# Two modulation spans of layer 2 computed by GpSimd and VectorE in place of TensorE

## The chip, the cores and the metric

One core of one Trainium2 chip runs the whole program in one launch. The metric is the time of an execution in microseconds, as the device measures it, of the slowest (here the only) core.

## The reference, cut to what matters

Four layers of a transformer-like block run one after another on 256 latent tokens and 256 context tokens, width 2048, in float32. In this text they are layers 0 to 3. Each layer is modulated by a condition vector:

```python
mod = jax.nn.silu(cond) @ w_ada[l] + b_ada[l]          # (2048) @ (2048, 6144)
shift, scale, gate = jnp.split(mod, 3, axis=-1)
h = rms_norm(x, norm_g[l]) * (1.0 + scale) + shift     # for latent and context tokens
p = h @ w_in[l]                                        # projections, attention, pooling, gates
x = x + gate * (merged(p) @ w_out[l])
```

There are two conditions for each layer (latent and context). Each third of a layer's w_ada, 2048 x 2048 numbers or 16.8 MB, is called a span here: span (2, 0) gives layer 2's shift, (2, 1) its scale, (2, 2) its gate. The modulation does not depend on x, so a span can be computed long before its layer begins. Layers 1 and 3 update only the latent tokens, so most of their projections run on 256 tokens; in layers 0 and 2 they run on 512.

## The kernel before, in words

**Slots.** All large weights pass through 500 slots of 128 x 1024 numbers (512 KB). SyncE's queue (SP) loads slot n into one of four w_raw buffers; ScalarE (`high`, line 732) copies it, rounded, to one of two w_high buffers; VectorE (`low`, line 1076) writes the rest, w_raw minus w_high, to w_low. TensorE forms each product as three matmuls (`three`, line 1670): high by high, low by high, high by low. While it computes slot n, the other two engines prepare slot n + 1. A w_high buffer is free when TensorE has used the slot two before (`slot_used`), so at the start of slot n ScalarE may begin on slot n + 1. A slot of 256 columns has 24 matmuls.

**Order.** `plan_phases` lists the phases of each layer, and every engine runs through the same list in its own program, in order. For layer 1 the slots are: q 120 to 135, kv to 143, cq to 151, ckv to 159, g_mla to 175, kr 176 and 177, g_gqa to 193, two short phases of the low-rank products to 207, then attention (mla) without slots, the splitting of its output (ysplit), and out 208 to 239. Beside cq, ckv and the first slot of g_mla runs another attention, one step a slot: TensorE scores, VectorE maximum, ScalarE exponential, VectorE weights, TensorE transposes and values. At the start of a layer (`root`, `apply`) VectorE scales x and writes h_low while TensorE begins on q. In out, each half round ends in a residual chain on VectorE: the update of x (line 1520), squares (1536), two sums (1542, 1550).

**Three forms for a span.** The modulation is done beside the slots in one of three forms, laid out by digits in the phases' lists.
- *Units* (`ada`, `span_unit`, line 1766): 16 units of 1 MB. For each, TensorE multiplies 4 x (128 x 512) numbers by the condition, and adds up in the PSUM bank `modulation` (AD). Units come in pairs behind the second and sixth slot of a round. `span_cols` (line 1775) turns the row into columns.
- *Mod pieces* (`mod`, `pieces`, lines 1120 and 1122): a span is two blocks of 16 pieces, 512 KB each. VectorE multiplies a piece by the condition and adds it to an accumulator, once for each of two conditions, two operations over 128 x 1024 a piece. At a block's end TensorE sums over partitions (`block_sums`, line 1787) and turns (`block_cols`, line 1821), ScalarE copies a row (line 752), VectorE adds the bias.
- *Gate pieces* (`gate`, `gate_pieces`, line 1140): the same for one condition only, one operation a piece.

Each queue is in order: SP loads piece p when VectorE has used piece p - 2, and the loads of later slots stand behind that wait. `TURNS` gives the bank AD to one owner at a time. In layer 1 before the change, q holds 8 units, kv and cq 4 each (span (2, 0)), and out 16 (span (2, 1)); kv, cq and ckv have 32 gate pieces. GpSimd only does the pooling of layers 2 and 3.

Of the kernel before, what the change touches and what calls it, by code (L numbers as in the profile page):

```python
# [8 lines left out]
P = 128  # L9
D = 2048  # L10
KC = D // P
S = 256
# [55 lines left out]
def plan_phases():  # L68
# [55 lines left out]
    for layer in range(LAYERS):  # L124
# [8 lines left out]
        if layer < 2:  # L133
            beside = 0 if layer == 0 else 1
            vec = (lambda m: m) if layer == 0 else (lambda m: "")
            late = (lambda m: m) if layer == 1 else (lambda m: "")
            linear("q", layer, 2, toks, "feat", "copy", "Q", heads=q_heads, ahead=5, ada=2 * beside,
                   mod=vec("0000000011111111"))
            linear("kv", layer, 1, ALL, "kv", "copy", "KV", ada=beside, mod=vec("11111210"), gate=late("11111111"), heads=all_stages({0: ("q", 3), 1: ("k", 0)}))
            att = attention(layer, 1, HD ** -0.5, 34, both)  # L140
            att["first"] = at["slot"]
            linear("cq", layer, 1, toks, "feat", "copy", "C", att=att, ada=beside, mod=vec("11111111"), gate=late("11111111"))
            linear("ckv", layer, 1, ALL, "feat", "copy", "C", att=att, off=2, mod=vec("11111111"), gate=late("22222222"))
            linear("g_mla", layer, 2, toks, "feat", "silu", "G", att=att, mod=vec("0111111111111111"))
            add("kr", layer=layer, att=att, mod=vec("10"))
# [3 lines left out]
            at["fd"] += 1  # L149
            linear("g_gqa", layer, 2, toks, "feat", "gate", "Q", sync=True, ranks="cq", mod=vec("1111121212111000"))  # L150

# [21 lines left out]
        else:  # L173
# [17 lines left out]
        add("ysplit", layer=layer, toks=toks)  # L191
        linear("out", layer, 4, toks, "feat", "res", "X", ada=4 if layer == 1 else 0, ahead=3,
               mod={0: "00011121121121110121121121121000", 2: "00000110110110111111121111111000"}.get(layer, ""))
# [14 lines left out]
def build(nc, dram, out):  # L208
# [7 lines left out]
    with ctx:  # L216
# [56 lines left out]
        pool_v = place("pool_values", [P, 2, PAD + S + PAD])  # L273
        pool_s = place("pool_sums", [P, 2, PAD + S + PAD])
        pool_edge = place("pool_edge", [P, 4, 2, 2, PAD])
        cols = place("gain_cols", [P, N_COLS])
# [33 lines left out]
        gate_used, gate_sum, gate_rowed = sem("gate_used"), sem("gate_sum"), sem("gate_rowed")  # L310
        gate_col, gate_ready = sem("gate_col"), sem("gate_ready")
        sq_done, ms_done, root_done = sem("sq_done"), sem("ms_done"), sem("root_done")
        scaled = sem("scaled")
# [41 lines left out]
        def columns_ready(layer, parts):  # L355

            if layer == 0 and parts == 2:
                return ada_ready, ADA_FIRST
            if (layer, parts - 1) in ADA_SPANS:
                return ada_ready, ADA_FIRST + ADA_SPANS.index((layer, parts - 1)) + 1  # L360
            if (layer, parts - 1) in GATE_SPANS:
# [109 lines left out]
        for ph in PH:  # L471
# [10 lines left out]
            for i in range(ph.get("ada", 0)):  # L482
# [3 lines left out]
                if span_of(q)[1] == 3:  # L486
                    TURNS.append((first, n0 + 8 * i + 8, "span", span_of(q)[0]))
        TURNS += [(n + 1, n + 3, "mod", b) for n, b in BLOCK_END.items()]
        TURNS.sort()
        for t, u in zip(TURNS, TURNS[1:]):  # L490
# [10 lines left out]
        def bank_free(kind, index):  # L501

            return turn_done(kind, index, dict(span=ada_ready, mod=mod_ready, gate=gate_ready))

        def row_free(kind, index):

            return turn_done(kind, index, dict(span=ada_col, mod=mod_col, gate=gate_col))

# [40 lines left out]
        def _(sp):  # L549
# [120 lines left out]
        def _(pool):  # L670
# [6 lines left out]
            def own():  # L677
                pool.wait_ge(own_pool, own_n[0])

            step(nc.gpsimd.memset(pool_v[:, :, :], 0.0))  # L680
            for ph in PH:
# [38 lines left out]
        def _(act):  # L720
# [24 lines left out]
            def block_row(n):  # L745
# [5 lines left out]
                act.wait_ge(mod_sum, b + 1)  # L751
                nc.scalar.copy(ada_row, AD[:, :]).then_inc(mod_rowed, 1)

            def gate_row(n):
# [181 lines left out]
            for pi, ph in enumerate(PH):  # L936
# [22 lines left out]
                elif kind == "linear":  # L959
# [41 lines left out]
                    def round_(i):  # L1001
# [3 lines left out]
                        for k in range(8):  # L1005
# [6 lines left out]
                            block_row(n0 + 8 * i + k)  # L1012
                            gate_row(n0 + 8 * i + k)
                            head_side(ph, 8 * i + k)
                            att_side(ph, n0 + 8 * i + k)
# [44 lines left out]
        def _(dve):  # L1060
# [81 lines left out]
            def gate_columns(n):  # L1142

                if n - 3 not in GATE_END:
# [288 lines left out]
            for pi, ph in enumerate(PH):  # L1433
# [37 lines left out]
                elif kind == "linear":  # L1471
# [95 lines left out]
                    def round_(i):  # L1567
# [3 lines left out]
                        for k in range(8):  # L1571
# [94 lines left out]
        def _(pe):  # L1666
# [112 lines left out]
            def block_sums(n):  # L1779
# [154 lines left out]
            for pi, ph in enumerate(PH):  # L1934
# [4 lines left out]
                elif kind == "linear":  # L1939
# [46 lines left out]
                    def round_(i):  # L1986
# [4 lines left out]
                        for k, (j, s) in enumerate(slot_plan(ph, i)):  # L1991
# [297 lines left out]
```

## Time and profile before

| | |
|---|---|
| median of 3 runs | 3003.23 us (2996.53 to 3004.24) |
| the profiled execution's own time | 3003.08 us |
| its span | 3001.3 us |
| its mean granted TensorE clock | 0.979 |
| TensorE busy | 2852.5 us (95%) |
| VectorE busy | 1910.9 us (64%) |
| ScalarE busy | 1024.4 us (34%) |
| GpSimd busy | 109.4 us (4%) |

The span is what the profiler saw from the first to the last instruction; the execution's time holds a little more around it. Engines stand in the rows as PE (TensorE matmuls), PEld (its weight loads), DVE (VectorE), ACT (ScalarE), POOL (GpSimd) and SP. A float32 matmul leaves two records. An arrow with an engine behind a time says what ended the wait.

### The profile page before, as it was taken

Reading aid. Unit: us, or ns where it says so; the run is one execution under the profiler, and the core shown is the slowest. Engines: PE = TensorE matmul, PEld = TensorE weight load, DVE = VectorE, ACT = ScalarE, POOL = GpSimd, SP = SyncE. Lnnn points to the kernel's source line nnn. Section 1 sums busy time; section 2 is a strip of 40 time slices with the busy share of each in tenths; the row PEclk is TensorE's granted clock in tenths of the full one; section 3 lists DMA queues with packets and bytes.
Section 4 is the critical chain, followed back from the end, with each engine's and each line's share of the span. In section 5 each row is a group of like instructions: output and inputs, shape, how many; then the busy total and the mean of one; then the engine's idle time right before and its main releaser. Section 6 shows DMA issues by size and latency. Waiting matters only on the chain.

```text
span 3001.3 us, 40313 instructions
## 1 busy us (share of the span) xinstructions
PE 2852.5 (95%) x16432; PEld 2350.3 (78%) x16432; DVE 1910.9 (64%) x2852; ACT 1024.4 (34%) x1515; POOL 109.4 (4%) x157
## 2 busy tenths in 40 slices
PE   6899999999998999999989999999999989999998
PEld 2588887786786888986877789767778877897888
DVE  3477677656887576455565577877576864538564
ACT  3223343225213233434332222334441232225463
POOL 0000000000000000000000000530000000004100
PEclk9999999999998999999999999999999989999999
DMA  9554344430555865434756755222534533322455
GB/s 404 233 175 163 122 153 143 159 116 36 180 199 178 288 228 183 160 114 143 275 189 234 265 212 183 104 91 106 181 120 156 182 111 123 97 92 91 151 180 169
DMA packets 145641, 501.90 MB, mean 167 GB/s; under 512 B 16048, under 2 KB 41392, under 8 KB 134960
## 3 DMA queue, kind: packets, MB, share of 16 engines
q1 hardware_dynamic: 136048, 489.65, 46.2%
q10 hardware_dynamic: 9408, 9.67, 0.9%
q8 instruction: 130, 2.13, 0.3%
q14 instruction: 55, 0.45, 0.1%
HBM read 484.05 MB, written 8.39 MB: 164 GB/s over the span
## 4 chain that ended last, share of the span: by engine, by line
PE 74%; DVE 8%; PEld 6%; issue 4%; DMA 3%; ACT 2%; POOL 1%; SPq 1%; PEldq 0%; DVEq 0%; ACTq 0%; POOLq 0%
PE products L1670 61%; PEld products L1670 5%; PE turned L1901 2%; DMA w_raw<-w_slots 2%; PE scores L1884 1%; DVE w_low L1076 1%; DVE tmp L1215 1%; PE modulation L1766 1%; ACT w_high L732 1%; DVE ada_w L1122 1%; PE products L1864 1%; DVE h_low L1243 1%; PEld turned L1901 1%; DMA mix_b<-ada_slots 1%; PE turned L1893 1%
## 5 line engine op out<-in xcount | busy, mean ns | idle before, releaser
L1670 PE MATMUL products<-h_high,w_high 128*128 128x512 f32 (+1 forms) x3424 | 1251.4, 365 | 84.3 <-DVE h_low L1243 33.0
L1670 PE MATMUL products<-h_low,w_high 128*128 128x512 f32 (+1 forms) x3424 | 1192.5, 348 | 0.0
L1670 PE MATMUL products<-h_high,w_low 128*128 128x512 f32 (+1 forms) x3424 | 1192.3, 348 | 0.0
L732 ACT CAST w_high<-w_raw 128x1024 fp32r<-128x1024 f32 x500 | 523.4, 1047 | 1327.0 <-PE products L1670 1135.9
L1076 DVE TENSOR_TENSOR w_low<-w_raw,w_high 128x1024 fp32r<-128x1024 f32 x500 | 614.5, 1230 | 557.5 <-ACT w_high L732 554.8
L1670 PEld LDWEIGHTS products<-h_high,w_high 128*128 128x128 f32 x3424 | 661.1, 193 | 254.7 <-issue 120.7
L1670 PEld LDWEIGHTS products<-h_low,w_high 128*128 128x128 f32 x3424 | 662.9, 194 | 79.4 <-issue 10.8
L1670 PEld LDWEIGHTS products<-h_high,w_low 128*128 128x128 f32 x3424 | 661.1, 193 | 81.1
L1122 DVE SCALAR_TENSOR_TENSOR ada_w<-ada_w,cond_silu 128x1024 f32<-128x1024 f32 x300 | 373.3, 1286 | 2.4 <-DMA ada_w<-mod_slots 0.7
L1670 PE MATMUL products<-w_high,h_high 128*128 128x256 f32 x640 | 183.3, 286 | 3.0 <-DVE w_low L1076 2.4
L1670 PE MATMUL products<-w_high,h_low 128*128 128x256 f32 x640 | 181.1, 283 | 0.0
L1670 PE MATMUL products<-w_low,h_high 128*128 128x256 f32 x640 | 181.1, 283 | 0.0
L891 ACT ACTIVATE tmp<-scores,softmax_stats,q_root 128x512 f32<-128x512 f32 (+1 forms) x144 | 101.4, 708 | 146.3 <-DVE softmax_stats L1363 146.3
L1670 PEld LDWEIGHTS products<-w_high,h_high 128*128 128x128 f32 x640 | 122.7, 192 | 7.5 <-issue 4.8
L1670 PEld LDWEIGHTS products<-w_high,h_low 128*128 128x128 f32 x640 | 122.8, 192 | 1.0 <-issue 1.0
L1670 PEld LDWEIGHTS products<-w_low,h_high 128*128 128x128 f32 x640 | 122.8, 192 | 0.0
L695 POOL COPY pool_values<-mix_a 128x512 f32<-128x512 f32 (+1 forms) x16 | 12.4, 773 | 2671.5 <-DVE mix_a L1509 2670.1
L1356 DVE TENSOR_REDUCE softmax_stats<-scores 128x1 f32<-128x512 f32 (+1 forms) x144 | 85.9, 597 | 30.1 <-PE scores L1881 19.2
L878 ACT COPY tmp<-turned 128x512 f32<-128x512 f32 (+1 forms) x96 | 49.3, 513 | 149.2 <-PE turned L1893 149.2
L810 ACT ACTIVATE h_high<-tmp,ada 128x256 fp32r<-128x256 f32 x128 | 57.5, 500 | 80.4 <-DVE tmp L1215 80.4
L1373 DVE RECIPROCAL softmax_stats<-softmax_stats 128x1 f32<-128x1 f32 x192 | 26.1, 157 | 65.5 <-ACT tmp L891 64.8
L1215 DVE SCALAR_TENSOR_TENSOR tmp<-x_residual,mod_scale,scores 128x256 f32<-128x256 f32 x128 | 55.2, 476 | 7.9 <-PE scores L1723 4.5
(232 smaller groups left out, 2698.7 us busy)
## 6 DMA issues: line engine op xcount, KB each, us to landing
w_raw<-w_slots SPq DMA_DIRECT2D x500, 512.0 KB, 3.7
ada_w<-mod_slots SPq DMA_DIRECT2D x160, 512.0 KB, 3.7
ada_w<-ada_slots SPq DMA_DIRECT2D x58, 1024.0 KB, 7.8
mix_b<-gate_slots SPq DMA_DIRECT2D x32, 512.0 KB, 4.0
mix_a<-gate_slots SPq DMA_DIRECT2D x32, 512.0 KB, 4.2
mix_a<-ada_slots SPq DMA_DIRECT2D x12, 1024.0 KB, 14.3
mix_b<-ada_slots SPq DMA_DIRECT2D x10, 1024.0 KB, 15.1
x_scratch<-x_residual ACTq DMA_DIRECT2D x3, 2048.0 KB, 9.1
```

Of the source, the lines that this page charges most:

```text
L732: nc.scalar.copy(whi[:, n % SPL, :], raw[:, n % RAW, :]).then_inc(high_done, 1)
L810: last = nc.scalar.activation(hh[:, t, tk], xs(t)[:, tk], ACT.Identity, bias=adaT[:, r, c + st:c + st + 1])
L878: nc.scalar.copy(dst[:, 0:nk], src[:, 0:nk]).then_inc(pt_done, 1)
L891: nc.scalar.activation(tmp[:, t0 + c % ring, 0:nk], src, ACT.Exp, scale=a["scale"] if a["wide"] else q_rs[:, k:k + 1], bias=stat[:, c % 8, ...
L1076: nc.vector.tensor_tensor(wlo[:, n % SPL, :], raw[:, n % RAW, :], whi[:, n % SPL, :].bitcast(F32), ALU.subtract).then_inc(low_done, 1)
L1122: ins = nc.vector.scalar_tensor_tensor(acc, w, c, acc, ALU.mult, ALU.add)
L1215: last = nc.vector.scalar_tensor_tensor(xs(t)[:, tk], xT[:, t, tk], mod_scale[:, t, st:st + 1], SC[:, 1, tk], ALU.mult, ALU.mult)
L1243: last = nc.vector.scalar_tensor_tensor(hl[:, t, tk], xs(t)[:, tk], adaT[:, r, c + st:c + st + 1], hh[:, t, tk].bitcast(F32), ALU.add, ALU ...
L1356: step(nc.vector.reduce_max(stat[:, c % 8, 0:1], src, AX.X))
L1670: ins = nc.tensor.matmul(o, a, b, start=first and q == 0, stop=last and q == 2, skip_group_check=skip)
L1766: ins = nc.tensor.matmul(AD[32 * j:32 * j + 32, :], sc32[:, k, :], place[:, j * 512:(j + 1) * 512], start=k == 0, stop=k == KC - 1)
L1901: ins = nc.tensor.matmul(o, v[:, kt, hc * HD:(hc + 1) * HD], pt[:, kt * P:(kt + 1) * P], start=kt == 0, stop=kt == nk // P - 1)
```

## The change

Span (2, 1), the scale, is computed by GpSimd through layer 1, in a new form called quiet: 64 pieces of 128 x 512 numbers (256 KB), which GpSimd loads from its own queue, two ahead. For each piece it forms two products and adds them to an accumulator in the half of mix_a that layer 1 leaves free (the first pieces only multiply). The first half of the pieces must be ready behind slot 173, the second behind slot 233, where TensorE sums and turns them. GpSimd begins when layer 1's h_low is complete. Span (2, 0), the shift, becomes 32 mod pieces of VectorE in kv, cq, ckv (5 each), g_mla (7) and g_gqa (10) of layer 1. Layer 1 has no unit left. SP waits for GpSimd's first half before it loads x in out. Cut to its core:

```diff
-ADA_SPANS = ((2, 0), (2, 1), (2, 2))
+ADA_SPANS = ((2, 2),)
-MOD_SPANS = ((0, 2), (1, 0), (1, 1), (3, 0), (3, 1))
+MOD_SPANS = ((0, 2), (1, 0), (1, 1), (2, 0), (3, 0), (3, 1))
+QUIET_SPAN = (2, 1)
+QUIET_PIECES = 2 * KC
+QUIET_END = {172: 0, 232: 1}
...
-            beside = 0 if layer == 0 else 1
-            linear("q", ..., ada=2 * beside,
+            linear("q", ...,
-            linear("kv", ..., ada=beside, mod=vec("11111210"), gate=late("11111111"), ...)
+            linear("kv", ..., mod=("11111210", "01101101")[layer], gate=late("11111111"), ...)
-            linear("cq", ..., ada=beside, mod=vec("11111111"), gate=late("11111111"))
-            linear("ckv", ..., mod=vec("11111111"), gate=late("22222222"))
-            linear("g_mla", ..., mod=vec("0111111111111111"))
+            linear("cq", ..., mod=("11111111", "01101101")[layer], gate=late("11111111"))
+            linear("ckv", ..., mod=("11111111", "01101101")[layer], gate=late("22222222"))
+            linear("g_mla", ..., mod=("0111111111111111", "0010101010101010")[layer])
-            linear("g_gqa", ..., mod=vec("1111121212111000"))
+            linear("g_gqa", ..., mod=("1111121212111000", "1101111011110000")[layer])
-        linear("out", ..., ada=4 if layer == 1 else 0, ahead=3,
+        linear("out", ..., ahead=3,
...
+                                    sp.wait_ge(quiet_added, 2 * (QUIET_PIECES - 2))
...
+            def quiet_load(p):
+                if p >= 2:
+                    pool.wait_ge(quiet_scaled, 2 * (p - 1))
+                if p == QUIET_PIECES:
+                    pool.wait_ge(gate_sum, 1)
+                nc.gpsimd.dma_start(quiet_w(p // QUIET_PIECES, p % 2), dram["quiet_slots"][p, :, :, :]).then_inc(quiet_landed[p % 2], 16)
+
+            def quiet_half(p):
+                b, chunk, h = p // QUIET_PIECES, p % QUIET_PIECES // 2, p % 2
+                cond = 2 * (QUIET_SPAN[0] // 2)
+                pool.wait_ge(quiet_landed[h], 16 * (p // 2 + 1))
...
+                for st in range(2):
+                    c = sc32[:, chunk, cond + st:cond + st + 1]
+                    nc.gpsimd.tensor_scalar(quiet_p(b, st), quiet_w(b, h), c, None,
+                                            ALU.mult).then_inc(quiet_scaled, 1)
+                if p + 2 < 2 * QUIET_PIECES:
+                    quiet_load(p + 2)
+                for st in range(2):
+                    acc = quiet_acc[:, st, h, :, :]
+                    pool.wait_ge(quiet_scaled, 2 * p + st + 1)
+                    nc.gpsimd.tensor_tensor(acc, acc, quiet_p(b, st), ALU.add).then_inc(quiet_added, 1)
...
+            def quiet_sums(n):
+                if n - 1 not in QUIET_END:
+                    return
+                b = QUIET_END[n - 1]
+                pe.wait_ge(quiet_added, 2 * (QUIET_PIECES - 2) * (b + 1))
+                pe.wait_ge(*bank_free("quiet", b))
+                for j in range(4):
+                    ins = nc.tensor.matmul(AD[32 * j:32 * j + 32, :].rearrange("p (t n) -> p t n", t=2), ONES[:, 0:32],
+                                           quiet_acc[:, j // 2, j % 2, :, :], start=True, stop=True)
+                ins.then_inc(quiet_sum, 1)
```

The turning into columns (`quiet_cols`), the row copy on ScalarE (`quiet_row`) and the columns on VectorE (`quiet_columns`) are those of a mod block.

## Rows read from the trace of the kernel before

**Rows 1.** The page's head: span, then busy time, share and instructions of an engine.
```profile
span 3001.3 us, 40313 instructions
...
PE 2852.5 (95%) x16432; PEld 2350.3 (78%) x16432; DVE 1910.9 (64%) x2852; ACT 1024.4 (34%) x1515; POOL 109.4 (4%) x157
```
**Rows 2.** The chain that ended last, share of the span by engine.
```profile
PE 74%; DVE 8%; PEld 6%; issue 4%; DMA 3%; ACT 2%; POOL 1%; SPq 1%; PEldq 0%; DVEq 0%; ACTq 0%; POOLq 0%
```
**Rows 3.** Windows by stage: stretch, its length, busy time of each engine, clock, DMA.
```profile
1169.00:1233.00 64.00, 63.47 (x476) 59.47 (x475) 29.21 (x32) 24.15 (x28) 0.00 (x0) 1.00 0.48 162
1233.00:1286.00 53.00, 51.94 (x403) 49.92 (x402) 26.58 (x32) 24.95 (x32) 0.00 (x0) 1.00 0.48 160
1412.00:1531.00 119.00, 111.91 (x884) 98.45 (x883) 67.12 (x78) 44.54 (x61) 0.00 (x0) 0.96 0.75 270
```
**Rows 4.** Timeline of ScalarE in g_mla: start, duration, idle time before it.
```profile
1197.62 1.05 ACT L732 CAST w_high<-w_raw 128x1024 fp32r<-128x1024 f32 x1 [1.83 <-PE products L1670]
1200.51 1.05 ACT L732 CAST w_high<-w_raw 128x1024 fp32r<-128x1024 f32 x1 [1.83 <-PE products L1670]
```
**Rows 5.** Timeline of VectorE in g_mla.
```profile
1198.70 1.23 DVE L1076 TENSOR_TENSOR w_low<-w_raw,w_high 128x1024 fp32r<-128x1024 f32 x1 [1.65 <-ACT w_high L732]
1201.59 1.22 DVE L1076 TENSOR_TENSOR w_low<-w_raw,w_high 128x1024 fp32r<-128x1024 f32 x1 [1.66 <-ACT w_high L732]
```
**Rows 6.** Timeline of TensorE in the short phase cq of layer 1.
```profile
1301.29 0.36 PE L1670 MATMUL products<-c_q_high,w_high 128*128 128x256 f32 x1 [1.02 <-DVE w_low L1076]
```
**Rows 7.** Groups of TensorE over the run: count, then busy time, mean ns, idle before.
```profile
L1766 PE MATMUL modulation<-ada_w,cond_silu 128*32 128x512 f32 x384 | 46.3, 600 | 0.0
...
L1787 PE MATMUL modulation<-ada_w,consts 128*32 128x512 f32 x80 | 10.7, 605 | 0.0
L1821 PE MATMUL modulation<-consts,tmp 128*128 128x4 f32 x80 | 9.5, 242 | 0.0
...
L1775 PE MATMUL modulation<-consts,tmp 128*128 128x16 f32 x24 | 2.9, 252 | 0.0
```
**Rows 8.** Waits of TensorE from 945 to 1015 us: total, times, longest.
```profile
PE products L1670 <- DVE w_low L1076: 6.6, 3, 3.0
PE products L1670 <- DVE h_low L1243: 3.9, 3, 2.3
```
**Rows 9.** Timeline of VectorE in out of layer 1, one residual chain.
```profile
1459.71 1.23 DVE L1536 TENSOR_TENSOR tmp<-x_residual 128x1024 f32<-128x1024 f32 x1
...
1462.71 2.35 DVE L1076 TENSOR_TENSOR w_low<-w_raw,w_high 128x1024 fp32r<-128x1024 f32 x2
```
**Rows 10.** Timeline of TensorE beside that chain: a pair of units, the next product.
```profile
1462.18 1.92 PE L1766 MATMUL modulation<-ada_w,cond_silu 128*32 128x512 f32 x16
1464.03 0.39 PE L1670 MATMUL products<-h_high,w_high 128*128 128x256 f32 x1
```
**Rows 11.** Timeline of VectorE in ckv: two gate pieces in a row.
```profile
1125.41 2.47 DVE L1140 SCALAR_TENSOR_TENSOR mix_b<-mix_b,cond_silu 128x1024 f32<-128x1024 f32 x2
```
**Rows 12.** Timeline of VectorE in cq: the ends of two successive slots.
```profile
1085.08 0.29 DVE L1395 COPY mix_a<-turned 128x128 f32<-128x128 f32 x1 [0.84 <-PE turned L1901]
...
1090.22 0.29 DVE L1395 COPY mix_a<-turned 128x128 f32<-128x128 f32 x1 [0.84 <-PE turned L1901]
```
**Rows 13.** Timeline of VectorE in layer 2, beside GpSimd's pooling.
```profile
1933.14 0.75 DVE L1384 SCALAR_TENSOR_TENSOR tmp<-tmp,softmax_stats 128x512 f32<-128x512 f32 x1
...
1937.31 3.28 DVE L1122 SCALAR_TENSOR_TENSOR ada_w<-ada_w,cond_silu 128x1024 f32<-128x1024 f32 x2
```
**Rows 14.** Timeline of GpSimd in the same stretch.
```profile
1931.09 1.04 POOL L701 TENSOR_TENSOR pool_sums<-pool_values 128x512 f32<-128x512 f32 x1
1932.22 1.50 POOL L706 TENSOR_SCALAR pool_values<-pool_sums 128x512 f32<-128x512 f32 x1
```
**Rows 15.** Groups of GpSimd, shapes kept apart: busy time, mean ns, idle before.
```profile
L706 POOL TENSOR_SCALAR pool_values<-pool_sums 128x512 f32<-128x512 f32 x4 | 7.2, 1788 | 0.3
...
L701 POOL TENSOR_TENSOR pool_values<-pool_sums 128x512 f32<-128x512 f32 x4 | 6.6, 1648 | 0.3
```
**Rows 16.** Groups of VectorE from 974 to 1221 us.
```profile
L1076 DVE TENSOR_TENSOR w_low<-w_raw,w_high 128x1024 fp32r<-128x1024 f32 x49 | 60.0, 1224 | 59.6 <-ACT w_high L732 59.2
L1140 DVE SCALAR_TENSOR_TENSOR mix_b<-mix_b,cond_silu 128x1024 f32<-128x1024 f32 x30 | 37.7, 1277 | 0.0
```
**Rows 17.** SP's issues of units: duration ns least, median, most.
```profile
L603 SPq DMA_DIRECT2D ada_w<-ada_slots x58: 327/328/1769, 4.3 to 1739.4; - x58
```
**Rows 18.** Timeline of VectorE: the last h_low of layer 1.
```profile
971.80 1.83 DVE L1243 SCALAR_TENSOR_TENSOR h_low<-tmp,ada,h_high 128x256 fp32r<-128x256 f32 x4
```

More of the change, by code:

```diff
@@ L149, in plan_phases @@
             at["fd"] += 1
-            linear("g_gqa", layer, 2, toks, "feat", "gate", "Q", sync=True, ranks="cq", mod=vec("1111121212111000"))
+            linear("g_gqa", layer, 2, toks, "feat", "gate", "Q", sync=True, ranks="cq", mod=("1111121212111000", "1101111011110000")[layer])
             def count_ranks():
@@ L191, in plan_phases @@
         add("ysplit", layer=layer, toks=toks)
-        linear("out", layer, 4, toks, "feat", "res", "X", ada=4 if layer == 1 else 0, ahead=3,
+        linear("out", layer, 4, toks, "feat", "res", "X", ahead=3,
                mod={0: "00011121121121110121121121121000", 2: "00000110110110111111121111111000"}.get(layer, ""))
@@ L274, in build, with quiet_w, quiet_p @@
         pool_s = place("pool_sums", [P, 2, PAD + S + PAD])
+        quiet_home = G[:, :, 0:S].rearrange("p (b t) n -> p b t n", t=2)
+        quiet_spare = pool_v[:, :, 0:S]
+        def quiet_w(block, half):
+            if block > 0:
+                return quiet_home[:, half, :, :]
+            return quiet_spare if half == 0 else xT[:, KC - 1, :].rearrange("p (t n) -> p t n", t=2)
+        def quiet_p(block, st):
+            if block > 0:
+                return quiet_home[:, 2 + st, :, :]
+            return xT[:, KC - 3 + st, :].rearrange("p (t n) -> p t n", t=2)
+        quiet_acc = Q[:, :, 0:S].rearrange("p (c h t) n -> p c h t n", c=2, h=2)
         pool_edge = place("pool_edge", [P, 4, 2, 2, PAD])
@@ L488, in build @@
         TURNS += [(n + 1, n + 3, "mod", b) for n, b in BLOCK_END.items()]
+        TURNS += [(n + 1, n + 3, "quiet", b) for n, b in QUIET_END.items()]
         TURNS.sort()
@@ L501, in bank_free @@
         def bank_free(kind, index):
[L503 removed]
+            return turn_done(kind, index, dict(span=ada_ready, mod=mod_ready, gate=gate_ready, quiet=quiet_ready))
         def row_free(kind, index):
[L507 removed]
+            return turn_done(kind, index, dict(span=ada_col, mod=mod_col, gate=gate_col, quiet=quiet_col))
         OUT_FIRST = {ph["at"]["mod"] // KC: ph["at"]["slot"] for ph in PH
@@ L680, in _ @@
+            pool.wait_ge(cond_ready, 1)
+            pool.wait_ge(y_low, KC)
+            pool.wait_ge(x_out, 16)
+            pool.wait_ge(part_low, next(PARTS[pi] for pi, ph in enumerate(PH)
+                                        if ph["kind"] == "apply" and ph["layer"] == 1) + KC)
+            quiet_load(0)
+            quiet_load(1)
+            for p in range(2 * QUIET_PIECES):
+                quiet_half(p)
+            pool.wait_ge(quiet_scaled, 4 * QUIET_PIECES)
             step(nc.gpsimd.memset(pool_v[:, :, :], 0.0))
@@ L752, in block_row, with quiet_row @@
                 nc.scalar.copy(ada_row, AD[:, :]).then_inc(mod_rowed, 1)
+            def quiet_row(n):
+                if n - 2 not in QUIET_END:
+                    return
+                b = QUIET_END[n - 2]
+                act.wait_ge(*row_free("quiet", b))
+                act.wait_ge(quiet_sum, b + 1)
+                nc.scalar.copy(ada_row, AD[:, :]).then_inc(quiet_rowed, 1)
             def gate_row(n):
@@ L1153, in gate_columns, with quiet_columns @@
                     adaB[:, r:r + KC].rearrange("p (b m) -> p b m", m=4), ALU.add).then_inc(gate_ready, 1)
+            def quiet_columns(n):
+                if n - 3 not in QUIET_END:
+                    return
+                half = QUIET_END[n - 3]
+                layer, part = QUIET_SPAN
+                r = layer * ADA_ROWS + part * KC + half * MOD_TILES
+                dve.wait_ge(quiet_col, half + 1)
+                src = AD[:, 0:16].rearrange("p (m c h) -> p m c h", m=4, c=2)
+                dst = adaT[:, r:r + MOD_TILES, :].rearrange("p (h m) c -> p m h c", m=4)
+                bias = adaB[:, r:r + MOD_TILES].rearrange("p (h m) -> p m h", m=4)
+                for st in range(2):
+                    last = nc.vector.tensor_tensor(dst[:, :, :, 2 * (layer // 2) + st], src[:, :, st, :], bias, ALU.add)
+                last.then_inc(quiet_ready, 1)
             def block_columns(n):
@@ L1789, in block_sums, with quiet_cols @@
                 ins.then_inc(mod_sum, 1)
+            def quiet_sums(n):
+                if n - 1 not in QUIET_END:
+                    return
+                b = QUIET_END[n - 1]
[5 more added lines that the diff above has]
+                ins.then_inc(quiet_sum, 1)
+            def quiet_cols(n):
+                if n - 2 not in QUIET_END:
+                    return
+                pe.wait_ge(quiet_rowed, QUIET_END[n - 2] + 1)
+                first = IDENT.rearrange("p (j r) -> p j r", j=4)[:, :, 0:1]
+                for m in range(4):
+                    ins = nc.tensor.matmul(AD[:, 4 * m:4 * m + 4], ada_row[:, m * P:(m + 1) * P], first,
+                                           start=True, stop=True)
+                ins.then_inc(quiet_col, 1)
             def gate_sums(n):
```

34 lines of the change are left out of this document (29 added, 5 removed).

## The prediction

> **What bounds the kernel now.** The page comes first: TensorE is busy for 95% of the span [rows 1], and it holds 74% of the chain that ended last [rows 2]. So an instruction taken off TensorE is worth its own time, unless something else is then late. The windows by stage of layer 1 say how much else there is: TensorE is busy for 63.5 of 64 us in the stretch of g_mla and for 51.9 of 53 in g_gqa, with VectorE at about half [rows 3]. What counts is VectorE's place inside a slot. A slot whose products have 256 columns takes 2.89 us: ScalarE's copies to w_high start at 1197.62 and 1200.51, each just after TensorE ends a slot [rows 4]. w_low, for the slot after, begins at 1198.70 and ends at 1199.93 [rows 5], some 0.5 us before TensorE wants it. Where VectorE has more to do, in the short stages, TensorE already waits 1.02 us for w_low [rows 6].
>
> **TensorE, removed.** Two spans are 32 units. A unit is 8 of the 384 records of line 1766, 46.3/48 = 0.96 us, so 30.9. Their column products: two of the three groups of line 1775, 2 x 0.97 = 1.9. Together 32.8 us [rows 7]. Part covers other waits. In q of layer 1 TensorE waits 3.9 us for h_low, which sets the pace of the first slots [rows 8]: the first pair of units (1.9 us) fills such a wait and gives nothing. In out of layer 1 the residual chain (squares from 1459.71, then two w_low from 1462.71, the first done at 1463.9 [rows 9]) is late in every round; TensorE runs a pair of units meanwhile, 1462.18 to 1464.03 [rows 10]. Without it, it waits 1.7 us, four times: 6.7. Left: 32.8 - 1.9 - 6.7 = **-24.2 us**.
>
> **TensorE, added.** Two mod and two quiet blocks, each summed and turned: (10.7 + 9.5)/10 = 2.0 us [rows 7], **+8.1 us**. Row copies and columns on ScalarE and VectorE are under 0.6 us each, beside slots; SP's queue moves the same 33 MB, half of it as 512 KB pieces, half from GpSimd's queue. I cost both at nothing, since the units' 1 MB loads go. On SP's queue a piece waits until VectorE has used the one two before it, and the w_raw loads stand behind that wait; a load leaves three slots ahead of its use, so a lag of one slot costs nothing and one of two would add to the sum.
>
> **VectorE, added: 32 pieces.** Two operations over 128x1024 take 2.47 us [rows 11]. Where they lie:
> - cq (5 pieces). A slot is 5.14 us, of which VectorE idles 0.84 [rows 12]. A piece overruns by 1.6 alone, 2.6 with GpSimd beside it (below); the lead of w_low takes up some 2 us. 5 x 2.0 - 2 = +8 (bounds 5 to 11).
> - kv and ckv (10 pieces): long slots, +1.5 (0 to 4).
> - g_mla (7): w_low, piece, w_low need 1.1 + 2.4 + 1.2 after a start 1.1 us into the slot. The second is late by 0.7, of which 0.5 is spare: 0.2 alone, 0.8 with GpSimd. +4 (1 to 6).
> - g_gqa (10, mostly in successive slots): 1.1 + 2.4 = 3.5 us of VectorE against 2.9 of TensorE: 0.7 a slot alone, 1.3 with GpSimd. +10 (7 to 13).
> Sum **+23.5 us**. The removed form cost VectorE nothing.
>
> **GpSimd beside VectorE.** Layer 2 shows it: a pair of 128x1024 operations took 3.28 us there [rows 13] against 2.47 [rows 11]. Beside GpSimd most such operations with both inputs in SBUF lose nothing and some 0.4 to 0.8; I take 0.2 each. In out of layer 1 each of eight residual chains has five of them and ends in a wait: 8 x 1.0 = 8, and three more where a longer wait drops the granted clock (0.96 in that stretch [rows 3]). **+11** (0 to 18). Ysplit and the remaining w_low: **+3** (0 to 6).
>
> **GpSimd itself.** A piece is two products and two additions of 128x512: 1.50 and 1.04 us with nothing in the way [rows 14], 2 x 1.50 + 2 x 1.04 + 4 x 0.08 = 5.4. Beside layer 2's VectorE they took 1.79 and 1.65 [rows 15]. In the stretch to slot 172 VectorE has some 113 us of two-input work (w_low 60.0, gate pieces 37.7 [rows 16], rotations and norms 15) and the change adds 21 pieces, 52 us: 165 of 247, a denser neighbour than layer 2's. I take 0.47 us of waiting an operation: 7.3 us a piece. It also issues its own load, which no row shows: SP's issues take 0.33 to 1.77 us [rows 17]; I take 1.0, the middle, as a 128-partition pattern of 1 KB runs is not the cheapest. 8.3 us a piece, the two of chunk 0 half of that: 30 x 8.3 + 2 x 4.2 = 257 us. It starts when layer 1's last h_low is done, 973.6 [rows 18], plus 4 us for the first load: ends at 1235. TensorE reaches the sums behind slot 173 at 1221 now; 15 us saved and 15 us added before it leave that. Late by 14, less what GpSimd gains once VectorE idles: **+13 us** (0 to 45). TensorE's queue is in order, so all behind it waits. The second block has 300 us for some 250: nothing. SP's wait before x is loaded is long past by then, and the memset and layer 2's pooling behind the quiet work on GpSimd's queue are wanted 350 us after it.
>
> The Trainium skill (DMA: Bandwidth & Descriptors) gives about 1 us for the first byte of a DMA from GpSimd's queue; no row here shows it, and by it the sum would stay as it is.
>
> **Sum**: -24.2 + 8.1 + 23.5 + 11 + 3 + 13 = +34.4 us. The profiled execution took 3003.08 us (span 3001.3, 1.8 around it), 0.15 below the median of the three runs: 3003.1 + 34 = **3037 us**.
>
> **Rivals.**
> 1. *The cover holds.* VectorE's idle half takes the pieces, GpSimd is in time: 3003.1 - 24.2 + 8.1 = 2987. For it: VectorE idles 1.66 us in such slots [rows 5]. Against: two neighbouring pieces need 7.0 us in 5.8. Chance 0.15.
> 2. *VectorE's excess alone*, GpSimd neither late nor in the way: cq 5, g_mla 1, g_gqa 7: 2987 + 13 = 3000. Against: the 3.28 us [rows 13]. Chance 0.10.
> 3. *GpSimd in time, but in the way*: the sum without 13, 3024. It is so if its own issue costs 0.5 us or less. Chance 0.17.
> 4. *GpSimd far behind* at slot 173. If issues cost the upper 1.77, 32 x 0.77 = 25 us more: 3062. If each of its operations shut VectorE's out for its whole length, 30 x 5.4 + 2 x 3 + 165 = 333 us of turns stand in 243: 90 late, not 13: 3114. For it: 3.28 against 2.47. Against: an operation with two inputs took its bare 0.75 us from 1933.14 [rows 13], while GpSimd's product ran 1932.22 to 1933.72 at its bare 1.50 [rows 14]. Chances 0.05 for the issues, 0.08 for the whole length. The Trainium skill (SBUF — State Buffer, Who interferes with whom) says that a VectorE instruction with two SBUF inputs and a GpSimd one that reads SBUF share a port, held for the whole instruction. By that rule the 3114 would come out; the trace agrees that they collide, and not that it is for the whole length.
> 5. Forecast, 3037: chance 0.45.
>
> Two runs of this kernel can be told apart from about 0.3%, 9 us. Faster by more: rival 1, 0.15. Within: rival 2 and the low edge of 3, 0.13. Slower: the rest, 0.72. The range leaves out half of rival 1's low side and the top of rival 4: 2988 to 3082. The forecast's own is 3015 to 3060.
>
> **What would show it.** TensorE's wait before the quiet sums at slot 173, on GpSimd, by 5 to 25 us (rival 3: none; rival 4: over 35); TensorE waiting for w_low 8 to 12 us in g_gqa and as much in cq, in steps of 0.7 to 1.3; residual chains of out an extra us long; w_low above 1.33 us in the mean through layer 1; GpSimd's piece at 7 to 9 us. I am wrong if g_gqa's slots stay at 2.9 us with pieces in them, or if GpSimd's first block ends before 1215.

## The result, and the profile after

The changed kernel takes 3092.67 us (median of 4 runs, 3088.23 to 3096.98), against 3002.84 us (4 runs, 2996.53 to 3004.24) for the kernel before: a ratio of 1.0304, 95% interval 1.0291 to 1.0317. That is 90 us slower. The prediction had the sign (3037 us, +34) and missed the size: 3092.67 lies above its range of 2988 to 3082.

First the page of the changed kernel: its head, the chain that ended last by engine, then two groups of VectorE.

```profile
span 3094.8 us, 40371 instructions
...
PE 2870.0 (93%) x16224; PEld 2376.0 (77%) x16224; DVE 2118.0 (68%) x2916; ACT 1024.8 (33%) x1517; POOL 589.0 (19%) x469
...
PE 62%; DVE 17%; PEld 6%; issue 5%; DMA 4%; ACT 3%; SPq 1%; POOL 1%; DVEq 0%; PEldq 0%; ACTq 0%; POOLq 0%
...
L1161 DVE TENSOR_TENSOR w_low<-w_raw,w_high 128x1024 fp32r<-128x1024 f32 x500 | 663.6, 1328 | 492.9 <-ACT w_high L807 489.6
...
L1207 DVE SCALAR_TENSOR_TENSOR ada_w<-ada_w,cond_silu 128x1024 f32<-128x1024 f32 x360 | 473.0, 1355 | 2.0 <-DMA ada_w<-mod_slots 0.2
```

Against [rows 1], TensorE has 208 matmul records fewer and is busy 17.5 us longer. VectorE is busy 207 us longer. GpSimd itself holds 1% of the chain, VectorE 17% where it held 8% [rows 2]. So GpSimd is hardly ever what the end waits for; VectorE is.

Next the windows by stage of layer 1, each from the first w_low of a stage to the first of the next: kv, cq, ckv, g_mla with kr, g_gqa, the low-rank phases with the attention behind them, and out. Columns: stretch, length, busy time of PE, PEld, DVE, ACT, POOL, then the granted clock, the DMA share and GB/s.

```profile
1008.40:1061.80 53.40, 49.33 (x310) 43.65 (x308) 52.11 (x37) 13.43 (x15) 50.07 (x31) 1.00 0.67 236
1061.80:1131.80 70.00, 46.41 (x258) 39.51 (x259) 66.32 (x67) 17.14 (x29) 65.80 (x41) 0.78 0.54 194
1131.80:1204.70 72.90, 65.04 (x309) 50.06 (x309) 67.71 (x76) 19.12 (x32) 68.81 (x42) 0.95 0.63 220
1204.70:1282.10 77.40, 70.06 (x507) 63.07 (x506) 59.87 (x53) 25.91 (x31) 53.42 (x37) 0.98 0.63 220
1282.10:1365.50 83.40, 60.64 (x404) 55.78 (x402) 78.94 (x54) 25.27 (x32) 78.75 (x48) 0.90 0.55 190
1365.50:1448.30 82.80, 71.44 (x437) 63.19 (x438) 68.38 (x55) 22.59 (x26) 77.32 (x56) 0.96 0.37 117
...
1448.30:1623.60 175.30, 154.89 (x1066) 134.46 (x1065) 109.24 (x165) 67.55 (x114) 56.57 (x44) 0.94 0.43 144
```

The kernel before, cut the same way, takes 49.3, 46.1, 60.7, 64.8, 52.2, 70.0 and 174.8 us. The changes are +4.1, +23.9, +12.2, +12.6, +31.2, +12.8 and +0.5; q, ahead of them, is 5.7 shorter. Their sum, 91.6, is the difference of the spans (93.5) to within 2 us. VectorE is busy 66 of 70 us in cq and 79 of 83 in g_gqa, and GpSimd as much. The clock is 0.78 and 0.90 there: part of these stretches ran at 1.2 GHz instead of 2.4, where before both had 1.00. Out is as long as before, but two changes cancel in it: its 16 units are gone, and GpSimd's work costs about as much (experiment 3).

What the operations of VectorE cost in layer 1, 974 to 1510 us (count, then busy time, mean ns):

```profile
L1161 DVE TENSOR_TENSOR w_low<-w_raw,w_high 128x1024 fp32r<-128x1024 f32 x84 | 152.1, 1811 | 30.1 <-ACT w_high L807 29.2 <-issue 0.5
L1207 DVE SCALAR_TENSOR_TENSOR ada_w<-ada_w,cond_silu 128x1024 f32<-128x1024 f32 x60 | 99.1, 1691 | 0.0
L1225 DVE SCALAR_TENSOR_TENSOR mix_b<-mix_b,cond_silu 128x1024 f32<-128x1024 f32 x30 | 45.8, 1545 | 0.4 <-DMA mix_b<-gate_slots 0.4
L1477 DVE TENSOR_SCALAR tmp<-tmp,softmax_stats 128x512 f32<-128x512 f32 x32 | 32.5, 1014 | 1.1
```

The first is 1.22 us and the third 1.28 without GpSimd [rows 16]; the second, the added pieces, takes 1.28 in the first experiment below, and the fourth 0.49 before. VectorE's excess over that: 84 x 0.59 + 60 x 0.41 + 30 x 0.27 + 32 x 0.53 = 99 us.

And TensorE's waits from 974 to 1540 us (total, times, longest), where the kernel before has 12.2 us for w_low and 1.7 for tmp:

```profile
PE products L1771 <- DVE w_low L1161: 42.1, 23, 5.9
PE turned L2025 <- ACT tmp L962: 15.4, 9, 3.8
PE turned L2017 <- DVE mix_a L1495: 9.2, 6, 3.1
PE scores L2005 <- issue: 7.7, 1, 7.7
```

None of them is for GpSimd. For the last, in cq, the profile names no releaser, but TensorE goes on just after VectorE has done its rotations and the copy to v_gqa. TensorE, then VectorE:

```profile
1072.50 2.04 PE L2005 MATMUL scores<-k_gqa,mix_a 128*128 128x512 f32 x2 [7.65 <-issue]
```
```profile
1071.19 1.21 DVE L1609 TENSOR_SCALAR v_gqa<-products 128x1024 f32<-128x1024 f32 x1
```

With GpSimd's work thinned (experiment 3) the same wait is 1.8 us. So some 6 us of cq's loss look like VectorE being late with the attention's inputs. Another place in cq shows how such a wait comes about. VectorE, GpSimd, ScalarE and TensorE, in that order:

```profile
1097.33 3.78 DVE L1161 TENSOR_TENSOR w_low<-w_raw,w_high 128x1024 fp32r<-128x1024 f32 x1
1101.03 0.68 DVE L1456 TENSOR_REDUCE softmax_stats<-scores 128x1 f32<-128x512 f32 x1
1101.74 0.21 DVE L1463 TENSOR_SCALAR softmax_stats<-softmax_stats,q_root 128x1 f32<-128x1 f32 x1
```
```profile
1096.71 0.75 POOL L713 DMA_DIRECT2D pool_values<-quiet_slots  x1 [0.30 <-POOL x_residual L736]
1097.49 2.52 POOL L743 TENSOR_TENSOR mix_a<-mix_a,x_residual 128x512 f32<-128x512 f32 x2
```
```profile
1101.99 0.78 ACT L975 ACTIVATE tmp<-scores,softmax_stats,q_root 128x512 f32<-128x512 f32 x1 [8.82 <-DVE softmax_stats L1463]
1102.67 0.19 ACT L975 ACTIVATION_READ_ACCUMULATOR tmp<-scores,softmax_stats,q_root 128x1 f32 x1
1102.76 0.57 ACT L962 COPY tmp<-turned 128x512 f32<-128x512 f32 x1
```
```profile
1103.39 1.86 PE L2025 MATMUL turned<-tmp,v_gqa 128*128 128x128 f32 x7 [3.40 <-ACT tmp L962]
```

A w_low of 1.22 us meets two additions of GpSimd, back to back for 2.52 us, and takes 3.78, their sum with its own to within 0.1 (its record even starts 0.16 us before the first addition's). The attention step's maximum stands behind it on VectorE, ScalarE's exponential waits for that, ScalarE's copy stands behind the exponential in its queue, and TensorE waits 3.4 us for the copy.

It is no single case. From 987 to 1508 us VectorE makes 79 w_low. 33 of them overlap an addition of GpSimd and take 2.62 us in the mean; what they take over 1.22 is on average 0.2 us less than that overlap. 23 lie, for nine tenths of their length or more, within GpSimd's products and take 1.29, at most 1.61.

### The profile page after: what moved, and what is told of

Same layout as the page of the kernel before. It is cut to its first block, busy times and chain, and to the rows that moved or that the text cites. A ratio compares the mean times of both kernels' runs of the same rounds, so it can differ in the third digit from the quotient of the medians.

```text
span 3094.8 us, 40371 instructions
## 1 busy us (share of the span) xinstructions
PE 2870.0 (93%) x16224; PEld 2376.0 (77%) x16224; DVE 2118.0 (68%) x2916; ACT 1024.8 (33%) x1517; POOL 589.0 (19%) x469
## 4 chain that ended last, share of the span: by engine, by line
PE 62%; DVE 17%; PEld 6%; issue 5%; DMA 4%; ACT 3%; SPq 1%; POOL 1%; DVEq 0%; PEldq 0%; ACTq 0%; POOLq 0%
PE products L1771 52%; PEld products L1771 5%; DVE w_low L1161 4%; DVE ada_w L1207 4%; DMA w_raw<-w_slots 2%; ACT w_high L807 2%; PE turned L2025 2%; PE scores L2008 1%; DVE tmp L1315 1%; SPq L616 1%; DVE mix_b L1225 1%; DVE h_low L1343 1%; PE products L1988 1%; PEld turned L2025 1%; DMA mix_b<-ada_slots 1%
## 5 line engine op out<-in xcount | busy, mean ns | idle before, releaser
L1161 DVE TENSOR_TENSOR w_low<-w_raw,w_high 128x1024 fp32r<-128x1024 f32 x500 | 663.6, 1328 | 492.9 <-ACT w_high L807 489.6
L1771 PEld LDWEIGHTS products<-h_high,w_high 128*128 128x128 f32 x3424 | 671.0, 196 | 283.4 <-issue 125.2
L1771 PEld LDWEIGHTS products<-h_low,w_high 128*128 128x128 f32 x3424 | 672.3, 196 | 80.5 <-issue 11.9
L1771 PEld LDWEIGHTS products<-h_high,w_low 128*128 128x128 f32 x3424 | 670.5, 196 | 81.0
L1207 DVE SCALAR_TENSOR_TENSOR ada_w<-ada_w,cond_silu 128x1024 f32<-128x1024 f32 x360 | 473.0, 1355 | 2.0 <-DMA ada_w<-mod_slots 0.2
L713 POOL DMA_DIRECT2D pool_values<-quiet_slots x16 | 12.2, 765 | 979.1 <-DVE h_low L1343 974.7
L736 POOL TENSOR_SCALAR mix_b<-mix_b,cond_silu 128x512 f32<-128x512 f32 x60 | 114.2, 1910 | 5.1 <-POOL mix_a L743 5.1
L1456 DVE TENSOR_REDUCE softmax_stats<-scores 128x1 f32<-128x512 f32 (+1 forms) x144 | 85.7, 595 | 23.4 <-PE scores L2005 12.6
L743 POOL TENSOR_TENSOR mix_a<-mix_a,x_residual 128x512 f32<-128x512 f32 x60 | 85.7, 1452 | 0.8
```

What stands on the lines that cost most here:

```text
L736: nc.gpsimd.tensor_scalar(quiet_p(b, st), quiet_w(b, h), c, None, ALU.mult).then_inc(quiet_scaled, 1)
L743: nc.gpsimd.tensor_tensor(acc, acc, quiet_p(b, st), ALU.add).then_inc(quiet_added, 1)
L1161: nc.vector.tensor_tensor(wlo[:, n % SPL, :], raw[:, n % RAW, :], whi[:, n % SPL, :].bitcast(F32), ALU.subtract).then_inc(low_done, 1)
L1207: ins = nc.vector.scalar_tensor_tensor(acc, w, c, acc, ALU.mult, ALU.add)
L1456: step(nc.vector.reduce_max(stat[:, c % 8, 0:1], src, AX.X))
L1771: ins = nc.tensor.matmul(o, a, b, start=first and q == 0, stop=last and q == 2, skip_group_check=skip)
```

## The experiments

Each was timed beside the kernel before: the first four against its 3004.18 us, the last four against 3001.62.

**Theory.** The loss is GpSimd's two-input additions holding VectorE off, in stages where the new pieces have taken VectorE's slack. **Rivals:** VectorE's pieces alone; GpSimd late at slot 173; the loads, SP's order and the blocks; GpSimd's products.

**1. The shift's pieces alone.** Span (2, 0) goes to VectorE's pieces as in the change, the scale span keeps its 16 units in out. Against the kernel before:

```diff
-ADA_SPANS = ((2, 0), (2, 1), (2, 2))
+ADA_SPANS = ((2, 1), (2, 2))
-MOD_SPANS = ((0, 2), (1, 0), (1, 1), (3, 0), (3, 1))
+MOD_SPANS = ((0, 2), (1, 0), (1, 1), (2, 0), (3, 0), (3, 1))
...
```

> The shift span alone goes to VectorE's mod pieces; the scale span stays 16 units of TensorE in out, GpSimd does no quiet work. Theory A (GpSimd's operations hold VectorE up, and this is most of the 90 us): only the bare excess of the pieces is left, some 13 us, against 14 us of TensorE work saved and 4 added: 3000 to 3012. Theory B (VectorE's 32 pieces overfill its slots by themselves): 3040 to 3060, TensorE waiting for w_low in g_gqa as long as in the changed kernel (some 20 us).

Measured: 3000.29 us, ratio 0.9986 (0.9974 to 0.9999). cq and g_gqa, the same stretches:

```profile
1050.90:1098.80 47.90, 40.71 (x295) 35.78 (x294) 45.46 (x67) 17.94 (x29) 0.00 (x0) 1.00 0.67 240
1226.90:1287.60 60.70, 54.76 (x415) 50.64 (x414) 49.45 (x53) 24.96 (x32) 0.00 (x0) 1.00 0.61 217
```

g_gqa is 8.5 us longer than before, so VectorE's bare excess is there, and the units taken away pay for it. Half of the change costs nothing. The clock stays at 1.00.

**2. GpSimd's span alone.** The scale span goes to GpSimd as in the change, the shift keeps its units in q, kv and cq. Against the changed kernel:

```diff
-ADA_SPANS = ((2, 2),)
+ADA_SPANS = ((2, 0), (2, 2))
-MOD_SPANS = ((0, 2), (1, 0), (1, 1), (2, 0), (3, 0), (3, 1))
+MOD_SPANS = ((0, 2), (1, 0), (1, 1), (3, 0), (3, 1))
...
```

> The scale span alone goes to GpSimd; the shift span stays 16 units of TensorE in q, kv and cq. Theory A: GpSimd slows VectorE in every stage of layer 1, but without pieces VectorE has room, so much is covered: 3020 to 3050, VectorE's operations with two inputs some 0.4 us longer in the mean beside GpSimd. Theory B: VectorE keeps its slack: 2990 to 3000. If the two halves add up, this and the mod-only kernel together lie 90 us above twice the kernel before; if they need each other (a full VectorE and a busy GpSimd), the sum is well below.

Measured: 3053.12 us, ratio 1.0155 (1.0126 to 1.0185), just above what was expected. cq and g_gqa:

```profile
1067.90:1121.60 53.70, 46.57 (x322) 38.23 (x320) 49.61 (x56) 18.67 (x30) 50.30 (x34) 0.94 0.76 277
1257.70:1327.60 69.90, 56.99 (x399) 53.97 (x398) 43.93 (x31) 24.70 (x32) 65.90 (x42) 0.93 0.46 151
```

The parts give -4 and +49, both together +90: 45 us arise only where the two meet. cq shows it best: +1.8 and +7.6 apart, +23.9 together.

**3. GpSimd thinned.** The changed kernel, but GpSimd's products and additions work on 16 of their 512 numbers (the products of a block's first pieces stay whole).

```diff
-                    nc.gpsimd.tensor_scalar(quiet_p(b, st), quiet_w(b, h), c, None,
+                    nc.gpsimd.tensor_scalar(quiet_p(b, st)[:, :, 0:8], quiet_w(b, h)[:, :, 0:8], c, None,
...
-                    acc = quiet_acc[:, st, h, :, :]
+                    acc = quiet_acc[:, st, h, :, :][:, :, 0:8]
...
-                    nc.gpsimd.tensor_tensor(acc, acc, quiet_p(b, st), ALU.add).then_inc(quiet_added, 1)
+                    nc.gpsimd.tensor_tensor(acc, acc, quiet_p(b, st)[:, :, 0:8], ALU.add).then_inc(quiet_added, 1)
```

> The changed kernel, but GpSimd's products and additions behind a block's first pieces cover 16 of their 512 numbers a partition (the rest of layer 2's scale is left out); loads, order and semaphores stay. Theory A: some 80 to 90 us go, 2998 to 3015, w_low back near 1.23 us. Theory B, or that the loads from GpSimd's queue are what costs: above 3050.

Measured: 2999.73 us, ratio 0.9984 (0.9973 to 0.9995). With every load, wait, place in a queue and block left as they are, 93 us are gone. So the loads, SP's order and the blocks are out as causes. Its page's head:

```profile
span 2994.9 us, 40371 instructions
...
PE 2831.8 (95%) x16224; PEld 2348.0 (78%) x16224; DVE 1983.3 (66%) x2916; ACT 1025.0 (34%) x1517; POOL 327.5 (11%) x469
```

This is the clean measure of what GpSimd's data does to the others. With the same instructions, the changed kernel's VectorE is busy 2118.0 - 1983.3 = 135 us longer; its TensorE is busy 2870.0 - 2831.8 = 38 us longer (the lower clock) and idle for 62 us more, which makes up the 99.9 us between the two spans. By stage, from q to out, experiment 3 takes 83.5, 45.2, 48.0, 59.8, 69.7, 61.1, 70.0 and 165.5 us. So GpSimd's data costs 1.7, 8.2, 22.0, 13.1, 7.6, 22.3, 12.9 and 9.8 us there, and out has its share.

**4. Another order.** The changed kernel with GpSimd's four operations as product, addition, product, addition, in place of two products and two additions.

```diff
-                if p + 2 < 2 * QUIET_PIECES:
-                    quiet_load(p + 2)
-                for st in range(2):
+                    if st == 1 and p + 2 < 2 * QUIET_PIECES:
+                        quiet_load(p + 2)
```

> The changed kernel with GpSimd's order product, addition, product, addition in place of product, product, addition, addition; same work. If two additions back to back shut VectorE out for both (waits of up to 2.5 us on one operation), parting them caps a wait at 1.3 us: longest w_low under 3 us, and 10 to 30 us off: 3060 to 3080. If only GpSimd's total time on the port counts, no change within 5 us of 3092.

Measured: 3076.75 us, ratio 1.0234 (1.0204 to 1.0263), 16 us below the changed kernel. w_low in layer 1 (duration ns least, median, most), then one of them beside GpSimd's addition:

```profile
L1160 DVE TENSOR_TENSOR w_low<-w_raw,w_high x88: 1207/1226/2645, 974.2 to 1507.3; 128x1024 fp32r<-128x1024 f32 x88
```
```profile
1114.50 2.57 DVE L1160 TENSOR_TENSOR w_low<-w_raw,w_high 128x1024 fp32r<-128x1024 f32 x1
```
```profile
1114.68 1.30 POOL L742 TENSOR_TENSOR mix_a<-mix_a,x_residual 128x512 f32<-128x512 f32 x1
1116.15 2.35 POOL L736 TENSOR_SCALAR x_residual<-x_residual,cond_silu 128x512 f32<-128x512 f32 x1 [0.17 <-POOL mix_a L742]
```

The longest w_low is 2.65 us (4.22 in the changed kernel), and 2.57 is 1.22 with one addition more. Yet VectorE's busy time stays high (2093.2 us): the holds are as many (33 w_low over 1.5 us in layer 1, against 30 in the changed kernel) and shorter. Splitting them helps by a sixth of the loss and no more.

**5. Additions thinned** to 16 numbers, products whole. The edit is the second and third of experiment 3.

> The changed kernel, GpSimd's additions cut to 16 numbers a partition (that part of layer 2's scale is left out), its products whole. Theory A1, the additions hold VectorE up (two inputs through the port, 1.3 us each, back to back) and the products only by 0.4 us each: 65 to 80 of the 93 us go, 3012 to 3030, longest w_low under 2.2 us. Theory A2, each operation costs by its length (products are 56% of GpSimd's time): 3035 to 3055.

Measured: 3005.94 us, ratio 1.0016 (1.0003 to 1.0029): below what was expected; 87 of the 93 us are gone. VectorE's w_low in layer 1, then VectorE and GpSimd in cq:

```profile
L1161 DVE TENSOR_TENSOR w_low<-w_raw,w_high x108: 1207/1224/1652, 975.3 to 1508.7; 128x1024 fp32r<-128x1024 f32 x108
```
```profile
1090.80 1.21 DVE L1161 TENSOR_TENSOR w_low<-w_raw,w_high 128x1024 fp32r<-128x1024 f32 x1
1092.77 2.47 DVE L1207 SCALAR_TENSOR_TENSOR ada_w<-ada_w,cond_silu 128x1024 f32<-128x1024 f32 x2
```
```profile
1088.90 4.54 POOL L736 TENSOR_SCALAR x_residual<-x_residual,cond_silu 128x512 f32<-128x512 f32 x2 [0.17 <-POOL mix_a L743]
```

The w_low from 1090.80 lies wholly inside GpSimd's pair of products and takes its bare 1.21 us. It is GpSimd that gives way: the pair takes 4.54 us, and one such product takes 1.55 at the least in the changed kernel.

**6. Products thinned**, additions whole. The edit is the first of experiment 3.

> The changed kernel, GpSimd's products cut to 16 numbers a partition (part of layer 2's scale is left out), its additions whole and back to back. A1: most of the loss stays, 3060 to 3085, w_low with waits up to 2.5 us. A2: 3035 to 3055.

Measured: 3077.87 us, ratio 1.0253 (1.0226 to 1.0280).

```profile
L1161 DVE TENSOR_TENSOR w_low<-w_raw,w_high x88: 1207/1225/4167, 975.4 to 1509.7; 128x1024 fp32r<-128x1024 f32 x88
```

The additions by themselves cost 78 us (against experiment 3), the products 6. On top of the other kind they cost 87 and 15. (The kernel before differs by 2.6 us between the two groups of runs, so these hold to some 3 us.) Either way the additions carry the loss. It is not for being the longer work: GpSimd's groups in the changed kernel, additions and then products (count, busy time, mean ns):

```profile
L743 POOL TENSOR_TENSOR mix_a<-mix_a,x_residual 128x512 f32<-128x512 f32 x60 | 85.7, 1452 | 0.8
L743 POOL TENSOR_TENSOR mix_a<-mix_a,mix_b 128x512 f32<-128x512 f32 x60 | 80.8, 1371 | 0.8
...
L736 POOL TENSOR_SCALAR mix_b<-mix_b,cond_silu 128x512 f32<-128x512 f32 x60 | 114.2, 1910 | 5.1 <-POOL mix_a L743 5.1
L736 POOL TENSOR_SCALAR x_residual<-x_residual,cond_silu 128x512 f32<-128x512 f32 x30 | 70.4, 2352 | 2.6 <-POOL mix_a L743 2.6
L736 POOL TENSOR_SCALAR x_residual<-pool_values,cond_silu 128x512 f32<-128x512 f32 x30 | 68.9, 2302 | 3.1 <-POOL mix_a L743 2.8 <-DMA pool_values<-quiet_slots 0.3
```

The additions are 166.5 us, the products 253.5. What in an addition makes the difference, its second input, its place in memory or the instruction itself, was not tested.

**7 and 8. The kernel before with its units moved**, to look for a version that beats both. In the changed kernel TensorE waits for w_low behind each residual chain of out. In the kernel before, a pair of units fills this wait in one half of a round. In the other half the pair stands one slot too late, and three waits of 2.35 us stay; one slot earlier it might fill them.

```diff
-        ADA_AFTER = (1, 1, 5, 5)
+        ADA_AFTER = (0, 0, 5, 5)
```

> The kernel before with one pair of units in each round moved from behind the second slot to behind the first. In out of layer 1 TensorE waits 2.3 us for w_low there in three of four rounds, and its clock falls after that; the pair (1.9 us) would fill the wait, as the other pair does now. If units can be had nearly free where VectorE is late: 3 x (1.9 + 1.6 of clock) = 10 us off, 2989 to 2997. If the wait is only moved behind the units: no change.

Measured: 2996.10 us over 12 runs, ratio 0.9977 (0.9967 to 0.9987). Out of layer 1, this kernel:

```profile
1356.00:1521.00 165.00, 157.78 (x1178) 127.73 (x1177) 97.05 (x163) 67.79 (x115) 0.00 (x0) 1.00 0.63 239
```

Of the three waits of 2.35 us one of 0.87 is left. Out falls from 174.8 to 165.0 us at a clock of 1.00 (0.97 before), but layer 2's q and k, which hold units too, give back 3.9: the span is only 5.2 us shorter. Experiment 8 is the same edit on experiment 1.

> The mod-only kernel (shift span by VectorE's pieces, scale span by 16 units in out) with the same move of one pair a round. Both gains would add: 3000 less 10, 2986 to 2993, the fastest so far.

Measured: 2998.51 us over 12 runs, ratio 0.9985 (0.9975 to 0.9995). It missed: the two gains do not add. Why was not followed further. Experiment 7 is the fastest kernel of this study by its median, 5.5 us below the kernel before. That is less than 0.3%, but the interval of 12 runs leaves out 1.

## Why the prediction was right in sign and wrong in size

**TensorE's share and VectorE's bare excess: right.** Rival 2 (VectorE's excess alone, GpSimd neither late nor in the way) was worked out as 3000 us. Experiment 3 makes just that case and takes 2999.73; experiment 1, with one of the two spans, takes 3000.29. The removal, the blocks, the waits that the units had covered and the pieces' 13 us all stand inside this sum. That the total is right could be luck, but its stages are right too. For cq the terms give +1.1 us (5 for the pieces, less 3.9 for four units), for g_mla +5 (1, and two blocks), for g_gqa +9 (7, and one block), for out -7.7 (16 units and one group of column products less 6.7 of waits and one block); experiment 3 has +1.9, +4.9, +8.9 and -9.3. g_gqa grew by 8.5 in experiment 1. And in out of the changed kernel TensorE waits where a pair of units ran [rows 10]; four such waits were foretold as 1.7 us, three stand there as 1.74, of which two:

```profile
1556.06 0.42 PE L1771 MATMUL products<-h_high,w_high 128*128 128x256 f32 x1 [1.74 <-DVE w_low L1161]
...
1586.68 0.39 PE L1771 MATMUL products<-h_high,w_high 128*128 128x256 f32 x1 [1.74 <-DVE w_low L1161]
```

**GpSimd beside VectorE: the step that failed.** Above 3000 the prediction had 37 us for GpSimd: 10.5 in the stages of pieces, 11 in out, 3 in ysplit and w_low, 13 for being late. It measured 93, most of it in other places.
- *The price of 0.2 us a two-input operation.* It was taken from layer 2, and came out at 0.59 for w_low, 0.41 for the new pieces and 0.27 for the gate pieces. Layer 2's GpSimd work is pooling; here the additions always come two back to back, and a VectorE operation that meets a pair waits for both. The bare 0.75 us beside a product [rows 13, 14], which the prediction read as a sign of mild contention, was a sign for products only: experiment 5 repeats it. The 3.28 us [rows 13] was the warning. What ran beside it were two additions:
```profile
1937.46 2.04 POOL L701 TENSOR_TENSOR pool_sums<-pool_values 128x524 f32<-128x524 f32 x1
```
  An addition took 1.06 us there with nothing in the way. This one starts 0.15 us after VectorE's pair and is some 1 us late, so there VectorE held GpSimd off first and was held afterwards.
- *What the delay turns into.* The prediction took it as overruns of a slot of w_low only. One-input work was hit too (0.49 to 1.01 us in the softmax), and through VectorE's and ScalarE's queues it reached the attention's matmuls: 15.4, 9.2 and 7.7 us of waits that had no term. TensorE's waits brought the clock down, 38 us of longer matmuls, for which only out had a term.
- *Slack is spent once.* Each part was priced against the slack of the kernel before. Experiments 1 and 2 show what that misses: -4 and +49 make +90. In experiment 2 VectorE is busy 114 us longer than before with the same instructions (2025.3 against 1910.9), nearly as much as the 135 of the changed kernel, and it costs about half: a VectorE that is half idle absorbs part of a hold, one that is full passes it on.

**GpSimd late at slot 173, +13: wrong, it was 20 us early.** Its own pace was priced well: 30 pieces from 987.16 to 1247.75 us are 8.7 us each, against 8.3. GpSimd around the end of the first half:

```profile
1245.04 2.71 POOL L743 TENSOR_TENSOR mix_a<-mix_a,x_residual 128x512 f32<-128x512 f32 x2
1268.22 4.25 POOL L725 TENSOR_SCALAR mix_a<-mix_b,cond_silu 128x512 f32<-128x512 f32 x2 [20.48 <-PE modulation L1900]
```

It ended at 1247.75, later than the 1235 foretold, but GpSimd then waited 20.5 us for TensorE's sums. TensorE, which the prediction expected at slot 173 by 1221, came some 46 us after that, delayed by the same additions. The prediction let the collisions act on GpSimd's pace and left TensorE's arrival as it was. The sign it named for itself, over 35 us of waiting under rival 4, did not appear at all; the price of the whole length was right for the additions, and the place where it would be paid was wrong.

**GpSimd in out, +11: the size by luck, the way wrong.** The stretch of out is 9.8 us longer in the changed kernel than in experiment 3. None of it comes from GpSimd beside the residual chains, where the 11 was put: its last addition starts at 1506.6, before them. 3.9 us lie in the attention ahead of out, beside GpSimd's last pieces. The other 5.9 come after it has ended (the changed kernel, then experiment 3):

```profile
1508.90:1623.60 114.70, 102.16 (x764) 99.68 (x764) 66.41 (x79) 42.48 (x56) 0.00 (x0) 0.91 0.46 155
```
```profile
1417.00:1525.80 108.80, 96.26 (x764) 93.53 (x763) 66.40 (x78) 43.72 (x60) 0.00 (x0) 0.97 0.49 163
```

TensorE waits the same 12.5 us for w_low in both, seven times, and is busy 5.9 us longer at a lower granted clock. Why the clock is lower there, with the same work and the same waits, no run shows. GpSimd's own issue, taken as 1.0 us, was 0.58 to 0.93, in most cases 0.60 or 0.75.

**The page's rule.** The Trainium skill (SBUF — State Buffer, Who interferes with whom) has a VectorE instruction with two SBUF inputs and a GpSimd one that reads SBUF share a port that is held for the whole instruction. For additions the traces agree, in 3.78 us against 1.22 + 2.52 and 2.57 against 1.22 + 1.30, to within 0.1. For products they do not: 1.21 us inside a pair of 4.54. The rival that was built on this rule, 3114 us, came nearer than the forecast by its price, not by its way: its 90 us were GpSimd's lateness, and GpSimd was early.

## What to carry to other kernels

A half-idle engine is not free room if its work holds off the engine that feeds the bottleneck: here GpSimd's work had to be priced by its kind (two-input additions at their whole length, doubled when two stand together), not by a mean over another mix. Count the slack of the victim after all parts of the change, since two parts that cost -4 and +49 us alone cost +90 together. To see quickly whether such a loss is data or order, thin the suspect's operands and keep its loads, waits and places: one run separated 93 us from all the rest. Compare stages with that run too, and not only with the kernel before: out looked untouched because a gain of 9.3 us hid a loss of 9.8.

## What the runs showed of the hardware

- GpSimd's addition of 128 x 512 (two inputs in SBUF) holds VectorE's two-input operation off for its whole length, and two back to back hold it for both: 1.22 us became 3.78, 4.22 at most, and the operation did not get in between. The 33 w_low that overlap an addition took 2.62 in the mean. With the additions apart the longest in layer 1 was 2.65. VectorE can hold an addition off too: the shortest took 1.26 us, the longest 2.31.
- GpSimd's product by a scalar (one input) lets it through and slows down itself: a pair took 4.54 us around a w_low at its bare 1.21. The 23 w_low within products took 1.29 in the mean, 1.61 at most. All products together cost 6 to 15 us of the run, all additions 78 to 87.
- VectorE's one-input multiply in the softmax was held too: 0.49 us in the mean before, 1.01 beside GpSimd. The 11 of 32 that overlap an addition took 1.78, 15 that overlap only products 0.67.
- TensorE's waits have a second price. In cq of the changed kernel it was busy 46.4 us for 258 records at a granted clock of 0.78, in experiment 1 40.7 us for 295 at 1.00. In the main part of out it was busy 102.2 us for 764 records at 0.91, in experiment 3 96.3 for the same number at 0.97; there the waits were equal, so they alone do not set the clock.
